# Two later waits for GpSimd's table loads in a fused transformer kernel

## What is computed

```python
mod = (c_act @ w_ada[l] + b_ada[l])[:, None, :]
sh1, sc1, ga1, sh2, sc2, ga2 = jnp.split(mod, 6, axis=-1)
h = rmsnorm(x, ln1_pre[l]) * (1.0 + sc1) + sh1
proj = h @ w_in[l]
q_a, k_a, v_a, q_h, f_h, i_h, g_h = jnp.split(proj, offsets, axis=-1)
attn = rmsnorm(swa_sink_alibi(q_a, k_a, v_a, attn_sinks[l]), attn_out_norm[l])
hg = hgrn2(q_h, f_h, i_h, lb_all[l])
...
mix = jnp.concatenate([attn, hg], axis=-1) @ w_out[l]
x = x + ga1 * rmsnorm(mix, ln1_post[l])
```

## Time and profile before

| | us |
|---|---|
| three runs | 2015.37, 2402.61, 2018.26 |
| their median | 2018.26 |
| the profiled execution | 2014.94 |
| its span in the trace | 2013.0 |
| TensorE busy in it | 1848.9 |

### The profile page before, as it was taken

One profiled execution on the slowest core, in us unless ns is written; L12 is line 12 of the kernel. 1 busy time (PEld: TensorE's weight loads), 2 busy tenths in 40 slices (PEclk: granted clock), 3 DMA queues, 4 the chain that ended last, 5 costly groups with the idle time before them and its releaser, 6 DMA issues.

```text
span 2013.0 us, 32223 instructions
## 1 busy us (share of the span) xinstructions
PE 1848.9 (92%) x13126; PEld 1244.8 (62%) x13127; DVE 864.4 (43%) x2029; ACT 544.0 (27%) x1037; POOL 458.9 (23%) x523
## 2 busy tenths in 40 slices
PE   6998999789888799999999999999999999999777
PEld 3777788654444588787666678456566555565432
DVE  3154634443222433624776324254444453444225
ACT  4142613311211342524676214011111111111102
POOL 1000000033221100012542000134444543454320
PEclk9999999889999899999999999999999999999998
DMA  9665631589999641153776143379999999999878
GB/s 374 252 247 182 237 126 63 189 329 417 416 417 409 238 148 63 63 126 97 153 138 129 63 178 126 142 304 405 395 372 410 411 411 377 408 396 410 330 271 355
DMA packets 103191, 532.31 MB, mean 264 GB/s; under 512 B 28082, under 2 KB 28386, under 8 KB 48380
## 3 DMA queue, kind: packets, MB, share of 16 engines
q1 hardware_dynamic: 64208, 457.73, 57.5%
q0 software_dynamic: 36256, 64.54, 11.8%
q10 hardware_dynamic: 2572, 7.81, 1.1%
HBM read 524.34 MB, written 51.90 MB: 286 GB/s over the span
## 4 chain that ended last, share of the span: by engine, by line
PE 75%; DMA 16%; DVE 4%; ACT 2%; issue 1%; SPq 0%; POOL 0%; ACTq 0%; POOLq 0%; DVEq 0%
PE ps L254 32%; PE ps L1764 18%; DMA arena<-in_egu 10%; PE ps L1838 9%; DMA arena<-in_ada 4%; PE ps L1733 3%; DMA arena<-y_rows 2%; PE ps L415 2%; PE ps L3162 1%; PE ps L1825 1%; PE ps L3188 1%; PE ps L2307 1%; PE ps L1088 1%; PE ps L1094 1%; DMA arena<-h_rows,arena 1%
## 5 line engine op out<-in xcount | busy, mean ns | idle before, releaser
L1764 PE MATMUL ps<-arena 128*64 128x256 f32 x4096 | 481.2, 390 | 47.0 <-DMA arena<-in_egu 39.0
L1764 PEld LDWEIGHTS ps<-arena 128*64 128x64 f32 x4096 | 298.3, 140 | 248.3 <-issue 64.0
L254 PE MATMUL ps<-arena 128*128 128x256 f32 (+4 forms) x1268 | 313.7, 405 | 8.9 <-DVE arena L1296 3.8
L254 PEld LDWEIGHTS ps<-arena 128*128 128x128 f32 (+1 forms) x1268 | 215.5, 191 | 91.3 <-issue 67.2
L1721 POOL DMA_INDIRECT y_rows<-arena x160 | 164.6, 1029 | 392.9 <-DVE arena L1874 249.8
L1838 PE MATMUL ps<-arena 128*64 128x512 f32 x1024 | 242.3, 602 | 7.5 <-DVE arena L1833 3.7
L1715 POOL DMA_INDIRECT arena<-h_rows,arena x160 | 170.5, 1066 | 272.9 <-DVE arena L1707 118.9
L1812 ACT ACTIVATE arena<-ps 128x256 f32<-128x256 f32 (+1 forms) x96 | 33.4, 348 | 662.1 <-PE ps L1764 662.1
L1833 DVE COPY arena<-ps 128x256 f32<-128x256 f32 (+1 forms) x96 | 36.5, 380 | 371.5 <-PE ps L1825 371.5
L3126 POOL DMA_DIRECT2D arena<-in_nabias x160 | 85.3, 541 | 283.5 <-PE ps L3004 156.3
L1838 PEld LDWEIGHTS ps<-arena 128*64 128x64 f32 x1024 | 66.3, 136 | 102.1 <-issue 97.1
(11 more groups left out here) (441 smaller groups left out, 2644.5 us busy)
## 6 DMA issues: line engine op xcount, KB each, us to landing
arena<-in_egu SPq DMA_DIRECT2D x204, 1024.0 KB, 14.4
arena<-in_ed SPq DMA_DIRECT2D x102, 1024.0 KB, 13.8
arena<-in_ada SPq DMA_DIRECT2D x48, 1024.0 KB, 7.0
arena<-in_win SPq DMA_DIRECT2D x37, 1024.0 KB, 5.1
arena<-y_rows SPq DMA_DIRECT2D x20, 1024.0 KB, 15.8
arena<-in_nabias POOLq DMA_DIRECT2D x96, 128.0 KB, 5.6
arena<-in_wout SPq DMA_DIRECT2D x8, 1024.0 KB, 6.9
h_rows<-arena ACTq DMA_DIRECT2D x8, 512.0 KB, 3.0
```

The lines of the kernel that those rows point to most:

```text
L254: z = pe.matmul(o, l, r, start=start and i == 0, stop=stop and i == len(pairs) - 1, skip_group_check=check)
L1764: z = pe.matmul(b[64 * j:64 * j + 64, 256 * s:256 * s + 256], XV[:, c, 64 * h:64 * h + 64], wk(k)[:, j * 256:j * 256 + 256], start=k == 0, ...
```

## The change

Two waits on GpSimd are set anew. `pool_first` now waits for the first half of modulation n = 5 (the sixth) in place of n = 3. `pool_rows1`, which had no wait, now waits for the first half of modulation n = 7 (the eighth). No load is added, removed or resized.

```diff
@@ pool_first
                     (iota128, a["iota128"]), (rope, a["rope"]), (ones, a["ones"])]
-            w.wait_ge(*ada.to("mm", 3, 0))
+            w.wait_ge(*ada.to("mm", 5, 0))
             for i, (dst, src) in enumerate(rows):
                 pool.dma_start(dst, src).then_inc(*ld.up("rows", "rows", i, by=16))
@@ pool_rows1
         def pool_rows1(pool, w):
+            w.wait_ge(*ada.to("mm", 7, 0))
             for i, (dst, src) in enumerate(((ALB, a["alibi"]), (LBR[:, 0:512], row("attn_norm")),
```

## The result

The changed kernel takes 2024.27 us (median of 9 runs, 2021.13 to 2027.91) against 2015.0 us for the kernel before, measured again beside it (9 runs). The ratio is 1.0043 with a 95% interval of 1.0031 to 1.0055: 9 us slower, clear of its noise and far within 2%. The first median of the kernel before, 2018.26, came from three runs; the further six lie between 2007.89 and 2017.21. One of its nine runs, 2402.61 us, stands apart and is left out of the ratio.

A forecast was written before the change was run, and what follows sets the result against it. TensorE, busy 92% of 2013.0 us, was taken as the bound, losing time where it waits. +1.5 (n=6) and +2.2 (n=8) give 3.7 us: 2018.6 from the profiled 2014.94, 2019.9 from the mean 2016.2; range 2012 to 2025.5.

The forecast's parts named there:

- n=5 free of waits, 6.7 us ahead: At n=5 the loads no longer meet the tables; block (p=1, q=0) starts at about 50.6 in place of 57.32.
- n=6's halves land at 61.5 and 65.3: At n=6, loads issued at U = 50.51, behind in_win for p=2, share DMA with 13 tables, landing at U+11.0 and U+14.8.
- TensorE 1.5 us behind after n=6: After n=6 the 6.7 us lead is spent and TensorE stands 1.5 us behind; bounds 0 and +2.8 with low clock.
- The wait at n=7 goes: At n=7 loads land by about 71, before TensorE comes at 72.6, so the 1.41 us wait disappears.
- n=8 loses 2.2 us, at most 4.4: At n=8 the three large loads delay the second half to T+12.8, T being in_win's issue for p=3; 2.2 us, bounds 0 to 4.4.
- The tables' users are far: Tables land 11 us before VectorE's constants at 75.57, the three large loads 14 us before the scores at 104.08.
- the surviving lead: Rival: tables transfer before SP's loads, n=6 ends 3.5 us ahead, n=8 loses nothing; -4.9 us, 2011 to 2013; chance 0.20.
- Nothing in sum: Rival: tables are hidden and the gain is lost to SP's wait for VectorE; within 1 us, 2015 to 2017; chance 0.20.
- 40 us slower: Rival: each of 18 modulations from n=6 on meets a wait over 3 us and the low clock, some 2.2 us each; chance 0.01.

The follow-up runs named there:

- e10: Changed kernel with SP issuing the two loads of each round's first modulation, from p=1, before in_win instead of behind it; one run, 2041.56 us against 2022.92.
- e3: Changed kernel with the three large loads waiting for the first half of n=8 instead of n=7; 2026.93 us against 2022.21 for the kernel before, ratio 1.0030.
- e6: Changed kernel with the three large loads waiting for the low part of w_in piece p=2 instead of n=7; one run, 2024.49 us.
- e2: Kernel before with only the three large loads moved, to wait for n=7, the 13 tables staying at n=3; 2025.95 us against 2022.21, ratio 1.0016.
- e11: Kernel before with only SP's order changed: two loads of each round's first modulation, from p=1, before in_win; one run, 2037.25 us.

## Why the prediction came out as it did

The forecast was 3.7 us slower, 2019.9 us, and the measured difference is 9.3. Direction and mechanism held: a lead, lost again for lack of free DMA time, with a second loss further on. The size was short by 6.3 us at the mark, in two terms. Both, 4.3 and 5.7 us, lie above the bounds that I had set for them, 2.8 and 4.4, and 9.3 lies above the 1 to 8 us that had the chance of 0.59. The time is inside the range by luck: the high end, 2025.5, puts both bounds on top of 2018.26, the highest undisturbed time shown; on top of the 2015.0 now measured they give 2022.2, below the 2024.27. (The low end's 2.9 does not come out of its words either: half of 4.9 is 2.45.)

1. *n=5 free of waits, 6.7 us ahead.* Right: transposes expected to end near 50.6, at 50.05 plus 0.66; block (p=1, q=0) ahead by 6.6.
2. *n=6's halves land at 61.5 and 65.3.* Right, at 61.84 and 65.42, and `e10` confirms the reason: SP's issue at 50.5. The sum behind it is in part luck: I had SP at 57.6% of the engines beside tables that come in at U+2.4; the tables moved from 50 us on, their first one landed in 2.2 us and not in 5.2, the two queues together held only 67% of 48 to 57 us, and SP held 69.5% of 53 to 62.
3. *TensorE 1.5 us behind after n=6.* Mis-sized: T came 4.3 us later. I had put the value between no loss and the low clock's +2.8, though the wait of 5.2 us that I had worked out myself was longer than the 3.27 us that had brought the low clock before. It also lasted longer than I had allowed: not only the half and the transposes, but the block of 24 behind them took 6.88 us in place of 5.76. In `e3`, the same program up to there, it took 5.55 us and T came 2.9 us later than before, next to the bound of 2.8; so 1.4 of the 4.3 us differ from one execution to the next.
4. *The wait at n=7 goes.* Right: 1.41 us to none.
5. *n=8 loses 2.2 us, at most 4.4.* This is the step that failed: from T to the mark it is 5.7 us. I had the second half land at T+12.8 and its matmuls end at T+13.9; it landed at T+15.5 and they ended at T+17.4. That is 2.7 us for the landing and 0.9 for the matmuls. First, I had GpSimd's transfers begin 1.5 us behind SP's, from the 5.2 us that the smallest table took to land; but that row was taken while the DMA engines were full. With empty engines GpSimd comes first. The DMA queues of the changed kernel, 77 to 82 us (packets, MB, share of 16 engines):

```profile
q0 software_dynamic: 175, 1.18, 75.2%
```

   SP's q1 has no row at all in this stretch, although SP issued 3 MB from 77.64 on; then, from 82 to 86 us, the shares are near those of the earlier trace rows:

```profile
q1 hardware_dynamic: 147, 1.12, 69.4%
q0 software_dynamic: 128, 0.40, 29.2%
```

   Second, that head start is at most 0.5 to 1 us of the mark (`e6`). The larger part is the weight: I reckoned 3.0 us for a share of 3.9. Fifteen of the second half's 16 parts had come by T+14.1, against T+9.8 for all of them before: 4.3 us, near the 3.9 us that the bytes take in quiet. So hardly any of their work hid behind SP's. Third, the last part came 1.3 us behind the other fifteen, as in `e3`; I had nothing for that. Fourth, the low clock: the half took 1.93 us in place of 1.07.

6. *The tables' users are far.* Right: no wait of VectorE for a table in either place.

Of the Trainium skill's rule ("DMA: Bandwidth & Descriptors", section "Queues, rings and completion order"), equal turns between queues, packet by packet: counted in the packets of the trace and where both queues were moving large loads, the trace agrees. From 82 to 86 us they moved 147 and 128 packets, in the earlier trace rows 249 and 220, and in `e6`, from 82.6 to 86.6 us, as good as the same number:

```profile
q0 software_dynamic: 110, 0.90, 53.2%
q1 hardware_dynamic: 111, 0.81, 48.0%
```

The shares of time, 69 to 29, differ because GpSimd's packets were smaller there (0.40 MB in 128, SP's 1.12 MB in 147). In the prediction I had compared the shares and said that the 67.4 to 33.8 of the earlier trace rows is not near equal turns; by packets it is. From 77 to 82 us the trace does not agree: 175 packets to none. The same is seen in `e2`, from 70 to 76 us:

```profile
q0 software_dynamic: 228, 1.34, 77.6%
q1 hardware_dynamic: 44, 0.36, 15.7%
```

There the measurement decides: a queue with 1 MB that finds the engines empty keeps them for some 4 us.

Of the rivals, the surviving lead would have needed the tables in front of SP's loads; they were issued from 49.41 on, 1.0 us before SP's, but one by one over 7 us, too thin to be through. Nothing in sum and 40 us slower did not come.

## What to carry to other kernels

A transfer that is taken out of one full stretch must be followed to where it lands: here 2.7 MB left a stall of 4.3 us and made two of 7.3 and 5.4 in stretches that had no stall. The share of busy DMA time doesn't say whether there is room (the 0.13 of 60 to 65 us stood behind a stretch with 1.01, and n=8's loads moved at 0.94); ask how many microseconds the next load that is waited for has to spare, counted from the instruction that lets it be issued. And a load that a queue can only issue late, because another stands in front of it, caps what any earlier gain can bring.

## What the runs showed of the hardware

- The first queue on empty DMA engines holds them: GpSimd issued 1.04 us ahead of SP and had 75% of the engines from 77 to 82 us, with SP's three loads without a packet until about 82. Issued 0.3 us behind SP, its 1 MB got its first packets about 4 us later and took 11.2 us to land in place of 5.4. The 13 small tables, 1.0 us ahead of SP, kept nothing back: SP's packets came within 1.5 us of its issue.
- Where both queues moved large loads, they moved nearly the same number of packets, not of bytes: 147 and 128, 249 and 220, 111 and 110. Beside the smallest tables it was 180 and 227.
- Waits of TensorE of 5.66 and 4.93 us, like the 3.27 us before, were each followed by matmuls of 1.93 us in place of 1.07, at the level of 1.2 GHz. In `e11` the same 3.27 us were followed by 16 matmuls of 1.07 us, and the low clock came behind the next wait, of 2.39 us. A wait of about 2 us did so in some executions and not in others: the 16 matmuls behind it took 1.07 us each time, but the block of 60 that followed took 9.66, 9.22 and 9.41 us behind waits of 1.96, 2.14 and 2.13 us, and 8.09 behind one of 2.16.
- Two loads and an `in_win` of 1 MB each landed 9.8 us behind the first issue in two kernels and 11.1 to 11.3 in four others. Fifteen of the 16 parts of the last load came at the same time in all six; the last one was 1.2 to 1.4 us late where a load of 16 KB of instructions had started by 9.1 us behind that issue, and on time where it started at 9.3. The link between the two is argued, not shown.
